# Running the four mixer units of a hybrid trunk in the order sample, prompt, sample, prompt

## What is computed

```
def trunk_layer(x, mod, p, ssd_h0, gdn_h0, kv_ctx):
    h = rmsnorm(x, p['norm1_w']) * (1.0 + sc1) + sh1
    u = h @ p['w_in']
...
    y = jnp.concatenate([y_ssd, y_gdn, y_fn, y_att], axis=-1) @ p['w_out']
    x = x + g1 * y
    h2 = rmsnorm(x, p['norm2_w']) * (1.0 + sc2) + sh2
    x = x + g2 * peer(h2, p['peer_w_q'], p['peer_keys'], p['peer_u'], p['peer_v'])
```

## Time and profile before

| | us |
|---|---|
| time, median of 3 runs (lowest, highest) | 3287.8 (3285.9, 3301.0) |
| the profiled execution: time, span | 3323.2, 3321.4 |
| PE busy | 1944.2 (59%) |
| DVE busy | 1769.2 (53%) |
| POOL busy | 1725.5 (52%) |
| ACT busy | 360.2 (11%) |
| DMA queue of the gathers: 805.40 MB | 66.9% of 16 engines |
| DMA queue of SP's weights: 142.62 MB | 11.4% of 16 engines |

### The profile page before, as it was taken

How to read it: one execution, slowest core, us unless ns; L and a number is a source line. 1 busy time by engine, 2 the same in 40 slices (tenths; PEclk the granted TensorE clock), 3 DMA queues, 4 the chain that set the end, 5 groups by cost and what they waited for, 6 DMA issues and landing times.

```text
span 3321.4 us, 27774 instructions
## 1 busy us (share of the span) xinstructions
PE 1944.2 (59%) x10194; PEld 1140.6 (34%) x10194; DVE 1769.2 (53%) x3951; ACT 360.2 (11%) x801; POOL 1725.5 (52%) x1540
## 2 busy tenths in 40 slices
PE   5888476657873321348878684676892000057787
PEld 4667365544642311331233163562660000001111
DVE  2423688862178988960013388873149888830000
ACT  2222111102111000000010011111210000000000
POOL 0000374434344777876545574444342877766665
PEclk9879687767996555679989996777896555579999
DMA  7557495546886998899999897546784999999998
GB/s 288 178 183 315 156 393 178 178 141 239 290 292 229 370 411 283 301 320 367 361 334 365 299 353 259 178 152 214 252 319 148 336 367 367 379 358 366 355 364 317
DMA packets 249064, 959.26 MB, mean 289 GB/s; under 512 B 32353, under 2 KB 33505, under 8 KB 231137
## 3 DMA queue, kind: packets, MB, share of 16 engines
q0 software_dynamic: 221184, 805.40, 66.9%
q1 hardware_dynamic: 19584, 142.62, 11.4%
q10 hardware_dynamic: 8160, 9.46, 0.8%
HBM read 955.01 MB, written 2.36 MB: 288 GB/s over the span
## 4 chain that ended last, share of the span: by engine, by line
POOL 25%; PE 25%; DVE 21%; DMA 13%; issue 13%; ACT 3%; ACTq 1%; another core or an unknown queue 0%; POOLq 0%; DVEq 0%
POOL sb_ring L486 25%; PE pb L509 16%; DMA sb_ring<-in_peer_v,sb_idxT 10%; PE pv L509 7%; DVE sb_ring L1803 6%; DMA sb_ring<-in_peer_u,sb_idxu 2%; PE pb L512 1%; DVE sb_pos L1715 1%; ACT sb_big L989 1%; DVE sb_big L1710 1%; ACT sb_hT L989 1%; DVE sb_big L1502 1%; DVE sb_big L1374 1%; DVE sb_big L1521 1%; DVE sb_big L1762 1%
## 5 line engine op out<-in xcount | busy, mean ns | idle before, releaser
L486 POOL DMA_INDIRECT sb_ring<-in_peer_u,sb_idxu x768 | 980.5, 1277 | 861.5 <-PE pv L509 399.1
L486 POOL DMA_INDIRECT sb_ring<-in_peer_v,sb_idxT x768 | 744.7, 970 | 714.9 <-PE pv L509 464.6
L1803 DVE CUSTOM_DVE_ANT_0 sb_ring<-sb_ring,sb_h 128x1024 f32<-128x1024 f32 x768 | 916.3, 1222 | 141.3 <-DMA sb_ring<-in_peer_u,sb_idxu 108.4
L509 PE MATMUL pv<-sb_ring,sb_wcol 128*32 128x512 f32 x3072 | 754.9, 646 | 174.4 <-DMA sb_ring<-in_peer_v,sb_idxT 139.6
L509 PE MATMUL pb<-sb_hT,sb_wring 128*128 128x256 f32 (+1 forms) x1920 | 383.7, 361 | 106.5 <-ACT sb_cinP L989 62.3
L509 PEld LDWEIGHTS pb<-sb_hT,sb_wring 128*128 128x128 f32 x1920 | 328.8, 207 | 180.8 <-issue 72.4
L509 PEld LDWEIGHTS pv<-sb_ring,sb_wcol 128*32 128x32 f32 x3072 | 134.5, 114 | 732.8 <-DMA sb_ring<-in_peer_v,sb_idxT 501.2
L509 PE MATMUL pb<-sb_big 128*128 128x128 f32 (+2 forms) x1888 | 257.4, 308 | 114.9 <-DVE sb_big L1502 80.6
L509 PEld LDWEIGHTS pb<-sb_big 128*128 128x128 f32 (+1 forms) x1888 | 250.4, 218 | 126.8 <-DVE sb_big L1502 85.6
L512 PE MATMUL pb<-sb_cst,sb_dots 128*128 128x128 f32 x6 | 2.7, 452 | 397.3 <-DVE sb_dots L1809 393.3
L1816 DVE COPY sb_accv<-pv 128x1024 f32<-128x1024 f32 x6 | 7.3, 1225 | 386.9 <-PE pv L509 373.7
(11 more groups left out here) (219 smaller groups left out, 1816.9 us busy)
## 6 DMA issues: line engine op xcount, KB each, us to landing
sb_wring<-in_w_in_blocks SPq DMA_DIRECT2D x32, 1024.0 KB
sb_ring<-in_w_mod_blocks SPq DMA_DIRECT2D x30, 1024.0 KB, 5.1
sb_wring<-in_w_q_blocks SPq DMA_DIRECT2D x27, 1024.0 KB
sb_wring<-in_w_mod_blocks SPq DMA_DIRECT2D x18, 1024.0 KB
sb_wring<-in_w_out_blocks SPq DMA_DIRECT2D x13, 1024.0 KB
sb_ring<-in_peer_u,sb_idxu POOLq DMA_INDIRECT x768
sb_ring<-in_peer_v,sb_idxT POOLq DMA_INDIRECT x768
sb_ring<-in_w_in_blocks SPq DMA_DIRECT2D x8, 1024.0 KB, 6.2
```

The costliest lines, as they stand in the source:

```text
L486: pool.indirect_dma_start(ring[:, j, :], None, a["tab_" + kind][l_of(q)], bass.IndirectOffsetOnAxis(ap=of, axis=0)).then_inc(rows_in[j], 16)
L509: return nc.tensor.matmul(out, lhsT, rhs, start=start, stop=stop)
L1803: dve.tensor_tensor_reduce(out=ring[:, j, :], in0=ring[:, j, :], in1=h2[:, t, :], scale=1.0, scalar=0.0, op0=ALU.mult, op1=ALU.add, accum_ ...
```

## The change

The four units run in another order: sample, prompt, sample, prompt in place of prompt, sample, prompt, sample. Layer 0 is still done before layer 1. `seq_tiles` gets the first numbers that fit: the sample of layer 0 is now q 0 and 1, the prompt q 2, and so on. Nothing else differs; `schedule()` makes the rest of it.

```diff
-UNITS = [(0, 0), (1, 0), (0, 1), (1, 1)]
+UNITS = [(1, 0), (0, 0), (1, 1), (0, 1)]
...
-    first = [0, 1, 3, 4][u]
+    first = [0, 2, 3, 5][u]
```

## The result

| | before | after |
|---|---|---|
| time, median (lowest, highest), us | 3292.1 (3285.9, 3301.0) | 3370.1 (3362.2, 3381.7) |
| ratio, 95% interval | | 1.0219 (1.0175 to 1.0262) |
| profiled execution: time, span, us | 3323.2, 3321.4 | 3377.8, 3376.1 |

The forecast was 3354 us in a range of 3318 to 3390: 66 us slower. The medians are 78 us apart, the two profiled executions 55.

What follows compares the result with a forecast made beforehand. Pieces with two tiles of experts follow the gathers (POOL itself in phase u beside a mixer); elsewhere engines wait along the chain. Exchanges +254, +194 and -381.5 sum to +66.5, scaled +66: 3354 us, range 3318 to 3390.

Steps and rivals of the forecast that it cites:

- P|2: Piece with the prompt mixer beside two tiles of experts: 865.4 us measured before; the new first one forecast at 852.
- S|1: Piece with the sample mixer beside one tile of experts: 658.0 and 658.9 us before, forecast 658.9 after.
- S alone: New opening piece, sample mixer with no experts beside it, in no trace: forecast 616 us, from 575 to 645.
- S alone for P alone: Exchange at the start: sample mixer without experts, 616 us, replaces prompt mixer without experts, 361.6: +254.
- two fifths of the dot products: Scan stage: of 87.7 us of dot products in S|1, 35 lie on the chain, so 237.0 becomes 202 without them.
- Fourier and attention ... 60: Stage of S alone: 98.2 us in S|1 less 36.4 of expert matmuls, less a wait, plus modulation blocks: 60.
- P|2 for S|1: Second exchange: 865.4 us less 13 gained at its start, 852 (780 to 870), in place of 658.0: +194.
- E1 for E2: Exchange at the end without mixer: one tile of experts, 396 us, in place of two, 777.5: -381.5.
- The other two pieces: One S|1 and one P|2 on both sides of the change: taken unchanged at 658.9 and 865.4 us.
- A: Rival: the new P|2 runs at the pace of the end without mixer, 758 us; sum -27, 3261 us; chance 0.04.
- B: Rival: more dot products on the chain, S alone 575 us or a little less; +25 or less, 3312; chance 0.11.
- C: Rival: ACT's modulation copies or a late block delay the scan, S alone 650; +100, 3387 us and more; chance 0.09.

## Why the prediction was right

The mechanism was right: the tile taken off the end gives back what was said, a P|2 costs more than an S|1 by nearly what was said, and the longer S alone is what makes the new order slower. In the first pair of profiles, S alone was 15 us over the forecast and P|2 14 under it. That the total came so close is in part luck.

**S alone for P alone**, +254 forecast, +270 and +258 in the two pairs of profiles. The first stage took 147.5 us in place of 141. The +8 for the second tile's load and the wider norm was right: where the first eight modulation blocks ran at the upper clock throughout (the kernel with no block in the last stages), the product with w_in began 8.0 us later than in P alone, and the stage took 140.8 at a granted clock of 0.94. In the changed kernel the last four of them ran at the lower clock, and their last fold came at 56.18 us in place of 49.58; the forecast had no term for that:

```profile
56.18 1.01 PE L509 MATMUL pv<-sb_cst,sb_modrow 128*128 128x2 f32 x4 [0.53 <-ACT sb_modrow L989]
```

An inverse was to take 44 to 45 us; PE's timeline has 47.1 for the first tile, at a granted clock of 0.93, and for the second 44.5.

The scan, 200 forecast, took 196.9. That the modulation blocks cost nothing there is right in the inverses, which held seven of the 16. It is wrong elsewhere: "as long as they fall into PE's waits" is a condition, and nine stand ahead of, between and behind the inverses. At 1.6 us each that is some 14 us, an estimate from the costs above. On the other side the two fifths of the dot products came from the inverse alone, and over the stage a half is nearer, 46 of 88 us in place of 35. The two small errors have opposite signs; that 200 came out is partly luck.

The term that was mis-sized is "Fourier and attention ... 60": 72.4. Without blocks the stage takes 56.2 us, so the rest of the term was sound; the blocks, priced at next to nothing there, cost 16.2. A block cost 1.6 to 2.0 us in this stage (64.2 us with five, 78.6 with eleven; in P alone 24.3 with none and 42.6 with nine), and at its start PE stood idle for 6.4 us. That a copy of ACT comes late there is not new: in P alone PE idles 8.1 us for one, behind other work of ACT. The wait for line 1344 is new: in P alone DVE came to that line early and waited for PE, in S alone the gated norm of two tiles stands ahead of it. The output product and the numbers, 133 and 82, measured 133.4 and 81.0.

**P|2 for S|1**, +194 forecast, +180 measured. The gain of 13 us at the start was about right: the first P|2 is 19 and 13 us shorter than the second in the two profiles. Its first use of a slot came 6.7 us after the first gather, against 26.6 in the earlier trace rows. What was too large is the 865.4 it was taken from: the other profile of before has 856.2. A gather of phase u takes 1.29 and 1.30 us over the two whole phases, not the 1.4 that was to be seen; the 1446 ns were read in 200 us of one phase.

**E1 for E2**, -381.5 forecast, -388 and -381 measured. **The other two pieces** stayed within 9 us, so the sign by which the method would have been wrong, over 10, was not seen. The tables' new place cost nothing that shows: S|1 is 660.3 and 662.5.

**The rivals.** A did not come about, but one argument against it was wrong. E2's 349 GB/s at 94% is no limit of DMA: with short dot products it moved 401 GB/s beside a mixer. The other argument decides: POOL takes 1.29 to 1.30 us a gather there, and once it doesn't, DVE is full. (The sum is zero at 785.5 us, not at 784.) The Trainium skill's rule ("SBUF — State Buffer", Who interferes with whom: a VectorE instruction with two inputs in SBUF contends with a GpSimd instruction that reads SBUF) agrees with the run: with one input in PSUM the gather is at 941 ns beside the mixer. I had counted the 1094 ns of E2 against the rule; with the tokens in PSUM E2's phase u has 936, so the rule holds there too. B and C did not come about; S alone lay between them. C's mechanism, ACT's copies of the modulation holding up PE, did occur, for 3.5 us. The range does not quite take in the lower bound of S alone, though the prediction says that it does: 3354 less 41 is 3313.

## What to carry to other kernels

Cut a pipelined program at the points where the same resource starts a new unit, check on two equal pieces that they last equally long, and price a new order as exchanges of pieces; only a piece that no trace contains needs an estimate by stages. An engine's idle share is not free room for side work as such. A filler is free where it stands just where the engine would wait, and costs its length, or more in a row with others, where the next step of the chain is ready behind it; it can also bring a wait of its own along. So place fillers one to a wait, and look at the timeline and not at the stage's average. A DMA share of 93 or 94% was no limit here, since 401 GB/s went through where it had been 341; lighten the engine that issues the transfers before calling the bytes the bound. And an engine's shorter instruction shortens a piece only if that engine bounds it: with gathers of 936 ns in place of 1126, E2 stayed what it was.

## What was not expected of the hardware

A gather's time on POOL, at the end with no mixer beside it, differs between kernels with the same instructions there. How gathers and line 1803 fall together may be the reason; no run shows it. These are the groups of phase u in E1 of the unedited kernel and of the one with all blocks in proj, output product and query, then phase u in E2 of the kernel before with no block in the attention:

```profile
L486 POOL DMA_INDIRECT sb_ring<-in_peer_u,sb_idxu x128 | 146.3, 1143 | 43.2 <-issue 39.6 <-PE pv L509 2.8 <-remote 0.8
```

```profile
L487 POOL DMA_INDIRECT sb_ring<-in_peer_u,sb_idxu x128 | 133.3, 1042 | 41.6 <-issue 38.4 <-PE pv L510 2.1 <-DVE sb_dots L1804 1.1
```

```profile
L488 POOL DMA_INDIRECT sb_ring<-in_peer_u,sb_idxu x256 | 268.6, 1049 | 96.5 <-issue 77.1 <-PE pv L511 18.6 <-DVE sb_dots L1805 0.8
```

With 1143 and 1042 ns the phase takes 187.0 and 173.1 us. In E2 the unedited kernel before has 1127 ns over both tiles, against 1049 here, and the phase takes 388.1 against 362.2 us. This can hide or feign a change of 0.8% elsewhere in the program, as it did for the kernel without blocks in the attention. The gather's length is not all of it: with the tokens in PSUM it is between 936 and 945 ns in all these phases, and still phase u of E1 takes 178.0 and that of E2 376.4 us, longer than the shortest ones here. What sets the rest stays open.
